# A decoder step on one core: its first modulation in two groups of feature blocks, the second tile ahead of the first keys, and the key work one slot later

## The chip, the cores and the metric

The kernel runs on one core of one Trainium2 chip. The metric is the device time of one execution in microseconds (us). The kernel before takes 1119.65 us, the median of three runs (1116.27 to 1120.73).

The engines are TensorE (PE; its weight loads are listed as PEld), VectorE (DVE), ScalarE (ACT), GpSimd (POOL) and SyncE (SP). Each works through its own queue in order and waits at semaphores for the others. SP, ACT and POOL issue the DMA transfers.

## The reference, cut to what matters

One step of a decoder with one layer, for a prompt (512 tokens) and eight sample sequences of four tokens each. The same weights serve both.

```python
def _modulation(c, w_mod, b_mod):
    m = jax.nn.silu(c) @ w_mod + b_mod            # 9 rows x 1024 @ 1024 x 6144
    return jnp.split(m[:, None, :], 6, axis=-1)

sh1, sc1, g1, sh2, sc2, g2 = _modulation(c, w_mod, b_mod)
h = _rmsnorm(x, norm1_w) * (1 + sc1) + sh1
z = h @ w_in                                      # 1024 x 3584
rq, rk, rv, rg, mq, mk, mv = jnp.split(z, SPLITS, axis=-1)
ret_out, ret_s = _retention_branch(...)
moba_out = _rmsnorm(moba_mix(mq, mk, mv), moba_norm_w)
x = x + g1 * (jnp.concatenate([ret_out, moba_out], axis=-1) @ w_out)
h2 = _rmsnorm(x, norm2_w) * (1 + sc2) + sh2
x = x + g2 * ((jax.nn.silu(h2 @ w_gate) * (h2 @ w_up)) @ w_down)
```

For the sample sequences, `moba_mix` reads a paged cache of 32 pages of 128 keys each: it scores the query against all keys, picks three blocks of 256 keys per query and weighs their values.

The shift `sh1` and the scale `sc1` (the first 2048 of the 6144 columns of `w_mod`) are needed before the first input matmul. The others are needed later.

## The kernel before, in words

Features lie on partitions: the 1024 features are eight blocks ("k") of 128. Weights come in chunks of 256 columns (1 MB). The main line of work is a row of tiles, each 128 output columns for all 512 prompt tokens: 28 tiles of the input projection (`half_tile`, twice per tile), 8 of the output projection, then the FFN. For precision each operand is split into a high and a low part, so a tile is 3 matmuls of 128x512 for each of the eight blocks: high by high and low by high weights (L1016, L1017) and high by low weights (L1018). ACT makes the high part (`split_hi`, `stage_hi`), DVE the low one (`split_in_place`, `act_lo`).

The order is written by hand on each engine, in slots: slot s goes with tile s (0 to 27), then come two slots, 30 to 42 the prompt's retention, 43 to 50 the output projection, 51 to 53 the second norm, from 54 the FFN. Each slot also carries one piece of the sample sequences' key work, on every engine: `slot_head(s)` multiplies key group s (`keys`, L1036; 64 groups, eight to a sequence), whose keys POOL gathers, and which DVE has turned (`turn_keys`, L1638); `slot_rest(s)` does what follows for the last finished sequence by s modulo 8: block sums (0), the choice of blocks (1), maxima (2), exponentials (3, `exps` on ACT), turned probabilities (3 and 4), folding of heads (4), denominators (5). Values of group g are weighed in slot g + `LAG`.

The first 2048 modulation columns are eight chunks of 256, computed one after the other through two buffers `raw[0]`, `raw[1]` (L386: SP loads a chunk once PE is done with the one that lay there). For a chunk PE accumulates block k in row group k % 4 of one bank, so that four partial sums of 32 rows lie below one another; `fold_groups` on DVE (L1549, L1551) adds them up with a copy and three additions. After two chunks `turn_mod` (L978) turns them, and `modulation` (L1562) adds the bias. `gains` (L1566) makes (1 + scale) x norm weight for all eight blocks at once. Only then does ACT stage x: PE turns x, which ACT has scaled by the inverse norm (L552), block by block (L991), and ACT applies gain and shift (L627), then makes the high part (L559); DVE makes the low one (L1594).

The two first sample chunks of the input projection (L961 with `asT`) come between blocks 1 and 2. PE then waits for the constants and starts slot 0 with `keys(0)`, which needs the sample queries out of those chunks (a transpose, `block_diagonal`, L1630) and key group 0; tile 0 comes behind it. The sixteen later modulation chunks go through `rawm` in the slots named in `MOD_AT`, and are turned in those of `TURN_AT`:

```python
MOD_AT = [0, 1] + list(range(2, NT, 2)) + [NT - 1]
TURN_AT = [2] + [MOD_AT[n] + 2 for n in range(3, len(MOD_AT) - 1, 2)] + [NT]
```

In the second norm (slots 51 to 53) DVE forms the reciprocal of the mean squares `rb` (L1958), ACT its square root (L851), and DVE and ACT scale and stage eight blocks in turn (L1950, L855). On ACT `slot(51)` stands ahead of a weight split and `slot(52)` between that and the square root.

## Time and profile before

| | before |
|---|---|
| median of three runs | 1119.65 us |
| the profiled execution | 1118.47 us, its span 1116.6 us |
| PE busy | 979.4 us (88%) |
| DVE busy | 656.7 us (59%) |
| ACT busy | 339.4 us (30%) |
| granted clock of PE, mean | 0.927 |
| moved by DMA | 267.01 MB, mean 239 GB/s |

Busy time is a share of the whole span, so it says little on one stage. The rows below give the stages: start times are in us from the span's start, and "idle before" is how long an engine stood before an instruction, with what released it. A granted clock of 1.00 is 2.4 GHz, 0.50 is 1.2 GHz.

### The profile page before, as it was taken

How to read it: one execution, taken by the hardware profiler on the slowest of the kernel's cores; microseconds unless marked ns; L12 is line 12 of the kernel's file. 1: busy time of each engine (PE TensorE's matmuls, PEld its weight loads, DVE VectorE, ACT ScalarE, POOL GpSimd, SP SyncE). 2: the span in 40 equal slices, each digit the busy share in tenths (PEclk: the TensorE clock that was granted, in tenths of full speed). 3: DMA queues.
4: the chain of work that ended last, by engine and by line, in shares of the span. 5: the costliest groups of instructions: out<-in, count | busy, mean ns of one | idle time of the engine just before them, and what ended most of it. 6: DMA issues, size and time to landing. Idle time of an engine off the chain costs nothing.

```text
span 1116.6 us, 20916 instructions
## 1 busy us (share of the span) xinstructions
PE 979.4 (88%) x7847; PEld 684.4 (61%) x7847; DVE 656.7 (59%) x1152; ACT 339.4 (30%) x678; POOL 91.0 (8%) x90
## 2 busy tenths in 40 slices
PE   3669999999999657467987699999999999999996
PEld 1356766766776334244753476767677777777775
DVE  3555775676676487776656657543266555553344
ACT  4331233324224324224214414333234222221113
POOL 0011110000010021101400123000000000000000
PEclk8679999999999788787988689999999999999998
DMA  9846878877777768576888567977847798887662
GB/s 294 303 150 232 309 252 280 294 263 265 272 261 261 229 229 307 189 257 208 267 300 281 188 212 249 276 226 227 272 123 216 193 233 236 226 242 237 202 227 80
DMA packets 220355, 267.01 MB, mean 239 GB/s; under 512 B 12785, under 2 KB 175929, under 8 KB 212066
## 3 DMA queue, kind: packets, MB, share of 16 engines
q1 hardware_dynamic: 111586, 123.21, 35.1%
q10 hardware_dynamic: 99456, 75.38, 22.0%
q0 software_dynamic: 9216, 67.11, 16.8%
q8 instruction: 62, 1.02, 0.4%
q14 instruction: 35, 0.29, 0.1%
HBM read 260.04 MB, written 5.64 MB: 238 GB/s over the span
## 4 chain that ended last, share of the span: by engine, by line
PE 73%; DVE 13%; DMA 5%; DVEq 3%; ACT 3%; issue 2%; SPq 1%; ACTq 0%
PE banks L1001 13%; PE banks L1002 12%; PE banks L1003 12%; PE banks L961 6%; PE banks L1016 4%; PE banks L1036 4%; PE banks L1091 4%; DVE KT L1638 4%; PE banks L1017 4%; PE banks L1018 4%; DMA raw<-in_w_mod 2%; PE banks L1179 2%; DVEq L1539 2%; DMA raw<-in_w_out 1%; PE banks L1164 1%
## 5 line engine op out<-in xcount | busy, mean ns | idle before, releaser
L1001 PE MATMUL banks<-ahi,whi 128*128 128x512 f32 x416 | 170.9, 411 | 0.0
L571 ACT ACTIVATE whi<-raw 128x1024 fp32r<-128x1024 f32 (+1 forms) x76 | 78.7, 1035 | 301.3 <-PE banks L1003 157.5
L1638 DVE STREAM_TRANSPOSE KT<-K 128x2048 f32<-128x2048 f32 x64 | 147.7, 2308 | 37.0 <-PE banks L1036 29.7
L1002 PE MATMUL banks<-alo,whi 128*128 128x512 f32 x416 | 164.2, 395 | 0.0
L1003 PE MATMUL banks<-ahi,rawlo 128*128 128x512 f32 x416 | 164.0, 394 | 0.0
L1601 DVE TENSOR_TENSOR rawlo<-raw,whi 128x1024 fp32r<-128x1024 f32 (+1 forms) x76 | 91.4, 1203 | 61.9 <-ACT whi L571 59.1
L478 POOL DMA_INDIRECT K<-in_cache_k,kidx x64 | 64.7, 1011 | 581.8 <-DVE KT L1638 538.2
L1001 PEld LDWEIGHTS banks<-ahi,whi 128*128 128x128 f32 x416 | 79.6, 191 | 31.5 <-issue 13.6
L1036 PE MATMUL banks<-KT,qbd 128*32 128x128 f32 x2048 | 75.2, 291 | 25.5 <-DVE KT L1638 24.2
L1016 PE MATMUL banks<-ahi,whi 128*128 128x512 f32 x224 | 93.6, 418 | 1.2 <-DVE rawlo L1608 0.9
L1003 PEld LDWEIGHTS banks<-ahi,rawlo 128*128 128x128 f32 x416 | 79.3, 191 | 17.7
L1002 PEld LDWEIGHTS banks<-alo,whi 128*128 128x128 f32 x416 | 79.9, 192 | 15.1
L1017 PE MATMUL banks<-alo,whi 128*128 128x512 f32 x224 | 88.7, 396 | 0.0
L1018 PE MATMUL banks<-ahi,rawlo 128*128 128x512 f32 x224 | 88.6, 396 | 0.0
L1036 PEld LDWEIGHTS banks<-KT,qbd 128*32 128x32 f32 x2048 | 57.7, 116 | 42.5 <-DVE KT L1638 20.9
L1091 PE MATMUL banks<-V,pT 128*32 128x512 f32 x368 | 54.0, 650 | 3.4 <-issue 2.0
L1016 PEld LDWEIGHTS banks<-ahi,whi 128*128 128x128 f32 x224 | 42.6, 190 | 18.3 <-issue 7.6
L1608 DVE TENSOR_TENSOR rawlo<-raw,whi 128x1024 fp32r<-128x1024 f32 x28 | 34.2, 1223 | 30.4 <-ACT whi L564 14.8
L655 ACT ACTIVATE pm<-banks,st 128x128 f32<-128x128 f32 (+3 forms) x32 | 16.6, 522 | 112.4 <-DVE st L1763 112.4
L1018 PEld LDWEIGHTS banks<-ahi,rawlo 128*128 128x128 f32 x224 | 42.8, 191 | 9.7
L1017 PEld LDWEIGHTS banks<-alo,whi 128*128 128x128 f32 x224 | 42.7, 191 | 7.7
L1551 DVE TENSOR_TENSOR xtmp<-xtmp,banks 32x256 f32<-32x256 f32 x90 | 37.5, 417 | 7.0 <-issue 0.4
(304 smaller groups left out, 1447.6 us busy)
## 6 DMA issues: line engine op xcount, KB each, us to landing
V<-in_cache_v SPq DMA_DIRECT2D x184, 256.0 KB
rawm<-in_w_mod ACTq DMA_DIRECT2D x15, 1024.0 KB
zT<-in_cache_v SPq DMA_DIRECT2D x52, 256.0 KB
raw<-in_w_in ACTq DMA_DIRECT2D x12, 1024.0 KB
raw<-in_w_gate ACTq DMA_DIRECT2D x22, 512.0 KB
raw<-in_w_up ACTq DMA_DIRECT2D x22, 512.0 KB
srw<-in_w_gate SPq DMA_DIRECT2D x22, 512.0 KB, 5.4
srw<-in_w_up SPq DMA_DIRECT2D x22, 512.0 KB, 6.7
```

The costliest lines, as they stand in the source:

```text
L571: act.activation(whi[t % 2][:, 0:kd, :], raw[u][:, 0:kd, t % 2 * P:(t % 2 + 1) * P], ACT.Copy).then_inc(s_hi, 1)
L961: last = pe.matmul(out[32 * g:32 * g + 32, 0:CHUNK], lhs(k), rhs[:, k, :], start=(first and k < 4), stop=(final and k >= kd - 4))
L1001: pe.matmul(out[:, :], whi[t % 2][:, k, :], hi(k), start=(first and n == 0), stop=False)
L1002: pe.matmul(out[:, :], whi[t % 2][:, k, :], lo(k), start=False, stop=False)
L1003: last = pe.matmul(out[:, :], low[:, k, :], hi(k), start=False, stop=(final and n == kd - 1))
L1016: pe.matmul(DB[:, :], whi[m % 2][:, k, :], ahi[:, k, :], start=(k == 0), stop=False)
L1017: pe.matmul(DB[:, :], whi[m % 2][:, k, :], alo[:, k, :], start=False, stop=False)
L1018: last = pe.matmul(DB[:, :], wlow[:, k, :], ahi[:, k, :], start=False, stop=(k == KT - 1))
L1036: last = pe.matmul(LG[32 * gq:32 * gq + 32, (g % 4) * P:(g % 4 + 1) * P], qbd[g // NGRP % 2][:, j, :], KTb[:, :, j, :], start=(jj == 0), s ...
L1091: pe.matmul(VO[32 * pg:32 * pg + 32, :], pT[:, n, 32 * pg:32 * pg + 32], bufs[pg][:, :], start=(n == 0), stop=(n == NGRP - 1)).then_inc(s_ ...
L1601: tt(rawlo[u][:, 0:kd, cols], raw[u][:, 0:kd, cols], whi[t % 2][:, 0:kd, :].bitcast(F32), ALU.subtract).then_inc(s_lo, 1)
L1638: dve.transpose(KTb[:, :, :, :], Kb[g % 2][:, :]).then_inc(s_kt, 1)
```

## The change

1. The first modulation is loaded in eight loads of two blocks k each. Loads 0 to 3 carry all 1024 features' rows for columns 0 to 511 of the shift and 0 to 511 of the scale; loads 4 to 7 those for columns 512 to 1023 of both. PE multiplies each load's two blocks by four groups of 256 columns, each group into its own 32 rows of one bank (bank 0 for the first four loads, bank 1 for the others), so no partial sums are left to fold. One copy and two transposes of 128x128 (`early_modulation`, `turn_early`) follow for each group of loads, and `gains` is called for blocks 0 to 3 and 4 to 7 separately.
2. Six of these loads have a buffer of their own (three new ones behind x, `rawm`, both `raw`) and are issued without a wait; the other two wait for loads 0 and 1 to be used. The sample rows are loaded ahead of x. Of x's four row blocks ACT scales two and DVE two.
3. PE turns x's blocks between the loads. Tile 0 takes high and low activations of each block as soon as it is staged, and the low weights at the end. Two modulation chunks (8 and 9) and tile 1 follow, ahead of `keys(0)`.
4. `KEYS = 1`: all key work comes one slot later on every engine; POOL's other work and the end of the sample sequences (`S_END`) are renumbered to match.
5. A later modulation chunk is kept with one copy of 128 rows; its four partial sums are added by PE as it turns them, through the constant `sum_pv`. `MOD_AT` has slot 0 twice and slot 27 no more.
6. Hidden units of the FFN lie in another order in the same two buffers, with their guards one slot later. Some semaphores of the sample retention are merged.

```diff
-LAG = 12
-MOD_AT = [0, 1] + list(range(2, NT, 2)) + [NT - 1]
+KEYS, LAG = 1, 12
+MOD_AT = [0, 0, 1] + list(range(2, NT - 1, 2))
+TURN_AT = [s + 2 for s in MOD_AT[1::2]]
-S_END = NG + LAG
+S_END = KEYS + NG + LAG
...
+    early = [at(ZT + 8192 + 2048 * i, f"early{i}", [P, 2, DM]) for i in range(3)]
+    mod_buffer = early + [two_k(rawm), two_k(raw[0]), two_k(raw[1])] + early[0:2]
...
+        def early_mod(n):
+            q, i = divmod(n, 4)
+            for a in range(2):
+                cols = slice(a * DM + q * 512, a * DM + q * 512 + 512)
+                sp.dma_start(mod_buffer[n][:, :, a * 512:(a + 1) * 512], w_mod_v[:, 2 * i:2 * i + 2, cols]).then_inc(EARLY[n][0], 16)
...
-        with sp.Fori(1, NMA // 2) as i:
-            for u in range(2):
-                sp.wait_ge(s_md, 2 * i + u - 1)
-                chunk(u, w_mod_v, bass.ds((2 * i + u) * CHUNK, CHUNK))
-        for u in range(2):
-            sp.wait_ge(s_md, NMA - 1 + u)
-            chunk(u, w_in_v, slice(COL_OF[u], COL_OF[u] + CHUNK))
+        for n in range(2, 6):
+            early_mod(n)
+        for n in range(6, NMA):
+            sp.wait_ge(s_md, n - 5)
+            early_mod(n)
+        sp.wait_ge(s_md, 5)
+        chunk(0, w_in_v, slice(COL_OF[0], COL_OF[0] + CHUNK))
+        sp.wait_ge(s_md, 6)
+        chunk(1, w_in_v, slice(COL_OF[1], COL_OF[1] + CHUNK))
...
+        def early_mod(n):
+            pe.wait_ge(*EARLY[n])
+            for kk in range(2):
+                for g in range(4):
+                    last = pe.matmul(bank[n // 4][32 * g:32 * g + 32, 0:CHUNK], cT[:, 2 * (n % 4) + kk, :],
+                                     mod_buffer[n][:, kk, CHUNK * g:CHUNK * (g + 1)],
+                                     start=(n % 4 == 0 and kk == 0), stop=(n % 4 == 3 and kk == 1))
+            last.then_inc(s_md, 1)
...
+        pe.wait_ge(s_hi, 1)
+        for k in range(KT):
+            pe.wait_ge(s_hlo, k + 1)
+            pe.matmul(DB[:, :], whi[0][:, k, :], ahi[:, k, :], start=(k == 0), stop=False)
+            pe.matmul(DB[:, :], whi[0][:, k, :], alo[:, k, :], start=False, stop=False)
+        pe.wait_ge(s_lo, 1)
+        for k in range(KT):
+            last = pe.matmul(DB[:, :], rawlo[0][:, k, 0:P], ahi[:, k, :], start=False, stop=(k == KT - 1))
+        last.then_inc(s_ft, 1)
+        mod_chunk(0)
+        mod_chunk(1)
+        half_tile(1, 0)
+        half_tile(1, 1)
         pe.wait_ge(s_const, 16)
-        for s in range(NT):
+        slot_head(1)
+        mod_chunk(2)
+        slot_rest(1)
+
+        for s in range(2, NT):
...
         def slot_head(s):
+            s -= KEYS
...
         def keep_mod(n, src):
-            dve.wait_ge(s_md, n + 1)
-            fold_groups(mst[0:32, CHUNK * (n % 2):CHUNK * (n % 2 + 1)], src, s_mev)
+            dve.wait_ge(s_md, NMA + n + 1)
+            then(cp(mst[:, CHUNK * (n % 2):CHUNK * (n % 2 + 1)], src[:, 0:CHUNK])).then_inc(s_mev, 1)
```

The first place where rows move is PE's queue between the modulation and tile 0. `raw_81` and `raw_82` are `raw[0]` and `raw[1]`, `cT` holds the turned conditioning vectors, `asT` the sample rows. Before:

```order
L961 MATMUL banks<-raw_82,cT 32x256 x8
L978 MATMUL banks<-ct,mst 128x32 x4
L1140 MATMUL banks<-ct,sq 128x32 x8
L991 MATMUL banks<-ct,xP 128x128 x8
L961 MATMUL banks<-raw_81,asT 32x256 x8
L961 MATMUL banks<-raw_82,asT 32x256 x8
L991 MATMUL banks<-ct,xP 128x128 x24
L1036 MATMUL banks<-KT,qbd_72 32x128 x16
L1016 MATMUL banks<-ahi,whi_85 128x512
```

The same place now, from the end of the first group of loads to tile 0:

```order
L1025 MATMUL banks<-ct,mst 128x128 x2
L1202 MATMUL banks<-ct,sq 128x32 x8
L1030 MATMUL banks<-ct,xP 128x128 x8
L1183 MATMUL banks<-raw_81,cT 32x256 x8
L1183 MATMUL banks<-raw_82,cT 32x256 x8
L1030 MATMUL banks<-ct,xP 128x128 x8
L1183 MATMUL banks<-early_95,cT 32x256 x8
L1030 MATMUL banks<-ct,xP 128x128 x8
L1183 MATMUL banks<-early_96,cT 32x256 x8
L1025 MATMUL banks<-ct,mst 128x128 x2
L1030 MATMUL banks<-ct,xP 128x128 x4
L993 MATMUL banks<-raw_81,asT 32x256 x8
```

The turns of x (L991, now L1030) have moved in among the loads of the second group, and a second pair of transposes (L1025) stands two blocks of x before the first sample chunk.

The second place is PE's queue from the end of tile 0 to tile 2 (`rawm` and `early_97` hold modulation chunks). Before, from tile 0's last matmul to the first of tile 1:

```order
L1018 MATMUL banks<-ahi,rawlo_83 128x512
L961 MATMUL banks<-rawm,cT 32x256 x8
L1036 MATMUL banks<-KT,qbd_72 32x128 x16
L1016 MATMUL banks<-ahi,whi_86 128x512
L1017 MATMUL banks<-alo,whi_86 128x512
```

Now tile 0's end and the beginning of tile 1:

```order
L1260 MATMUL banks<-ahi,rawlo_83 128x512 x8
L993 MATMUL banks<-rawm,cT 32x256 x8
L993 MATMUL banks<-early_97,cT 32x256 x8
L1053 MATMUL banks<-ahi,whi_86 128x512
L1054 MATMUL banks<-alo,whi_86 128x512
```

And tile 1's end and the beginning of tile 2:

```order
L1055 MATMUL banks<-ahi,rawlo_83 128x512
L1073 MATMUL banks<-KT,qbd_72 32x128 x16
L993 MATMUL banks<-rawm,cT 32x256 x8
L1073 MATMUL banks<-KT,qbd_72 32x128 x16
L1053 MATMUL banks<-ahi,whi_85 128x512
```

Key groups 0 and 1, which stood before tiles 0 and 1, stand together before tile 2, with one modulation chunk between them.

The third place is ACT's queue in the second norm, with what each row waits for (`rb` is the root of the mean squares, `pe_x` are the sample exponentials, `whi` a weight chunk's high part). Before:

```order
L846 ACTIVATE stage_55<-x2T 128x512 [waits x2_sums,tile_evicted+2]
L595 ACTIVATE pe_x,sm<-lgs,sm 128x4x32 [waits probs_turned,exp_bias]
L595 ACTIVATE pe_x,sm<-lgs,sm 128x4x32 x7
L599 ACTIVATE sm<-sm 128x32
L588 ACTIVATE lgs<-banks 128x512 [waits exps,logits]
L571 ACTIVATE whi_85<-raw_82 128x1024 [waits tile_done+2,w_loaded1]
L607 ACTIVATE pT<-banks 128x128 [waits page_used,probs_turned]
L607 ACTIVATE pT<-banks 128x128 x3
L851 ACT_TABLE_LOAD
L851 ACTIVATE rb<-rb 128x512 [waits x2_inverse]
```

Now:

```order
L874 ACTIVATE stage_55<-x2T 128x512 [waits x2_sums,tile_evicted+2]
L594 ACTIVATE whi_85<-raw_82 128x1024 [waits tile_done+2,w_loaded1]
L618 ACTIVATE pe_x,sm<-lgs,sm 128x4x32 [waits probs_turned,exp_bias]
L618 ACTIVATE pe_x,sm<-lgs,sm 128x4x32 x7
L622 ACTIVATE sm<-sm 128x32
L611 ACTIVATE lgs<-banks 128x512 [waits exps,logits]
L879 ACT_TABLE_LOAD
L879 ACTIVATE rb<-rb 128x512 [waits x2_inverse]
```

The weight split now comes before the exponentials, and nothing but the copy of the logits is left between them and the square root. The copies of the turned probabilities (L607) have moved behind the third staged block.

## Rows read from the trace of the kernel before

**Rows 1.** The page's slices: 40 equal parts of the span, PE's busy tenths.

```profile
PE   3669999999999657467987699999999999999996
```

**Rows 2.** Short windows: busy us of PE, PEld, DVE, ACT, POOL, clock, DMA share, GB/s.

```profile
6.00:8.00 2.00, 0.00 (x0) 0.00 (x0) 0.00 (x0) 0.00 (x0) 0.00 (x0) 1.00 1.08 354
48.00:50.00 2.00, 2.00 (x25) 0.80 (x17) 1.36 (x3) 0.81 (x2) 0.00 (x0) 0.64 1.05 429
58.00:60.00 2.00, 0.62 (x3) 0.22 (x2) 1.21 (x2) 1.97 (x4) 0.00 (x0) 0.50 0.00 0
```

**Rows 3.** The chain of waits, 0 to 180 us: start, us, what.

```profile
15.39 7.44 DMA raw<-in_w_mod
...
32.60 6.35 DMA raw<-in_w_mod
...
75.53 7.04 DMA rawm<-in_w_mod
```

**Rows 4.** Timeline, 0 to 100 us: start, us, engine, line, operation, count, idle before.

```profile
17.97 1.06 ACT L542 ACTIVATE sq<-xP 128x1024 f32<-128x1024 f32 x1
...
25.50 4.25 ACT L552 ACTIVATE xP<-xP,st 128x1024 f32<-128x1024 f32 x4
...
39.00 1.94 PE L961 MATMUL banks<-raw,cT 128*32 128x256 f32 x16 [0.99 <-DMA raw<-in_w_mod]
...
41.49 1.40 DVE L1551 TENSOR_TENSOR mst<-mst,banks 32x256 f32<-32x256 f32 x3
...
44.02 0.23 DVE L1566 SCALAR_TENSOR_TENSOR gain<-mT,vT 128x72 f32<-128x72 f32 x1 [0.15 <-issue]
...
46.07 0.78 ACT L627 ACTIVATE stage<-banks,mT,gain 128x512 f32<-128x512 f32 x1 [0.69 <-PE banks L991]
...
60.80 0.69 DVE L1594 TENSOR_TENSOR alo<-stage,ahi 128x512 fp32r<-128x512 f32 x1 [0.64 <-ACT ahi L559]
...
63.37 2.31 DVE L1638 STREAM_TRANSPOSE KT<-K 128x2048 f32<-128x2048 f32 x1
...
67.69 0.80 PE L1016 MATMUL banks<-ahi,whi 128*128 128x512 f32 x1
...
74.39 1.07 PE L961 MATMUL banks<-rawm,cT 128*32 128x256 f32 x16
...
76.27 0.50 PE L1016 MATMUL banks<-ahi,whi 128*128 128x512 f32 x1
...
82.08 0.60 ACT L633 ACTIVATE zT<-banks 128x512 f32<-128x512 f32 x1 [4.96 <-PE banks L1018]
...
95.83 0.50 PE L1016 MATMUL banks<-ahi,whi 128*128 128x512 f32 x1
```

**Rows 5.** PE's waits by releaser, 76 to 160 us: total, times, longest.

```profile
PE banks L961 <- DVE mst L1551: 1.9, 1, 1.9
```

**Rows 6.** The same, 300 to 400 us.

```profile
PE banks L978 <- DVE mst L1551: 2.7, 1, 2.7
```

**Rows 7.** The chain of waits, 530 to 700 us.

```profile
553.85 16.70 DMA raw<-in_w_out
...
571.84 3.27 DVEq L1644
```

**Rows 8.** Timeline of ACT and of DVE in the second norm.

```profile
599.55 0.51 ACT L595 ACTIVATE pe_x<-lgs,sm 128x128 f32<-128x128 f32 x1
...
602.63 0.30 ACT L599 ACTIVATE sm<-sm 128x32 f32<-128x32 f32 x1
...
605.35 1.28 ACT L851 ACT_TABLE_LOAD   x1
...
606.64 0.63 ACT L851 ACTIVATE rb<-rb 128x512 f32<-128x512 f32 x1
...
605.40 1.23 DVE L1601 TENSOR_TENSOR rawlo<-raw,whi 128x1024 fp32r<-128x1024 f32 x1
...
608.41 1.29 DVE L1950 TENSOR_TENSOR stage<-x2T,rb 128x512 f32<-128x512 f32 x2
```

More of the change, by code:

```diff
@@ L96, in constants @@
     put("pad0", np.zeros((P, 6)))
+    put("sum_pv", (p % 32)[:, None] == np.arange(32)[None, :])
     put("ones", np.ones((P, P)))
@@ L1134, in slot_rest, with turn_x_early @@
                 fold(b - 1)
-        pe.wait_ge(s_xsn, 1)
-        for k in range(KT):
-            last = pe.transpose(DB[:, k * S:(k + 1) * S], sq[0:S, k * P:(k + 1) * P], ident[0:S, 0:S])
-        last.then_inc(s_xst, 1)
-        pe.wait_ge(s_xn, 1)
-        for k in range(KT):
+        def early_mod(n):
[6 more added lines that the diff above has]
+            last.then_inc(s_md, 1)
+        def turn_x_early(k):
             if k >= 2:
@@ L1588, in _, with early_modulation @@
-        dve.drain()
-        gains(8, V_N1)
+        def early_modulation(group):
+            dve.wait_ge(s_md, 4 * group + 4)
+            then(cp(mst[:, CHUNK * group:CHUNK * (group + 1)], bank[group][:, 0:CHUNK])).then_inc(s_mev, 1)
+            dve.wait_ge(s_mtp, group + 1)
+            for h in range(2):
+                pick = lambda x: x.rearrange("p (a q k h) -> p a q k h", a=2, q=2, k=2)[:, :, group, :, h]
+                dst = mT[:, 0:16, :].rearrange("p (a q k h) s -> p a q k h s", a=2, q=2, k=2)[:, :, group, :, h, :]
+                last = then(tt(dst, SB[:, h * P:(h + 1) * P].rearrange("p (a k r) -> p a k r", a=2, k=2)[:, :, :, 0:NSEQ],
+                               pick(vT[:, 0:16]).unsqueeze(3).broadcast_to((P, 2, 2, NSEQ)), ALU.add))
+            last.then_inc(s_mp, 1)
@@ new lines, in _ @@
+        dve.reciprocal(st2[0:S, 12:13], st2[0:S, 12:13])
+        dve.drain().then_inc(s_rin, 1)
+        dve.wait_ge(s_rst, 1)
+        for i in range(2, TT):
+            last = ts(xP[:, i, :], xP[:, i, :], st2[:, i:i + 1], None, ALU.mult)
+        last.then_inc(s_xn, 1)
+        early_modulation(0)
+        gains(0, 4, 8, V_N1)
+        dve.wait_ge(s_pt, 16)
+        dve.wait_ge(s_ident, 16)
+        for g in range(GRP):
+            q = slice(32 * g, 32 * g + 32)
+            last = ts(kidx[q, :], pt[q, :].rearrange("p (n g) -> p n g", g=GRP)[:, :, g], 32.0, C("row32")[q, :], ALU.mult, ALU.add)
@@ L1591, in act_lo @@
+        last.then_inc(s_idx, 1)
         def act_lo(k, n):
```

302 lines of the change are left out of this document (167 added, 135 removed).

## The prediction

> **What bounds the kernel now.** I read the slices of the span first. TensorE (PE) is at nine tenths or more almost everywhere, except in the first three slices, in a valley in slices 14 to 19 and in slices 22 and 23 [rows 1]. So only work that shortens the time before PE fills up, or those two valleys, can move the end; the change is in the first 100 us.
>
> There the short windows show what is idle. The DMA engines are full while a load is queued (354 GB/s with share 1.08 at 6 to 8 us, 429 at 48 to 50), but stand at share 0.00 at 58 to 60, where PE works 0.62 of 2.00 us at the lower of its two clocks, granted 0.50 [rows 2]. The chain of waits says what that beginning consists of: waits for modulation loads (7.44 and 6.35 us, and 7.04 for a later one), since a buffer is refilled only after PE has used it [rows 3]. Then the timeline shows an almost serial path: last modulation chunk at 39.00, four fold additions, gain at 44.02, staging of feature block 0 at 46.07, block 7's low part at 60.80, the first key transpose at 63.37, tile 0 at 67.69, tile 1 at 76.27, tile 3 at 95.83 [rows 4]. My milestone is the start of tile 3: after it both programs run the same work in nearly the same order.
>
> **The start, step by step.** All from rows, kept apart by engine.
>
> *Loads.* They are the same bytes (eight of 1.05 MB), now six in flight without a wait. Small loads, x and four of them are 6.75 MB: at 354 GB/s from 3 us on that is 3 + 19.1 = 22.1, with half a us to land 22.6. All eight: 10.95 MB, 33.9. Both input chunks, constants, two more modulation chunks and two key gathers: 17.7 MB, 53.0 at 354 and 49.8 if what follows 33.9 runs at 429; I take 51. The Trainium skill (DMA: Bandwidth & Descriptors, "Where 436 GB/s comes from") gives both ends a name: a fabric ceiling of 435 GB/s and a share of about 358 of the HBM for one core. The trace has windows at either number [rows 2]; by the first alone the last of the 17.7 MB would land at 49.5, by the second alone at 52.8; the sum holds neither.
>
> *First group.* x's squares started at 17.97, behind those of the sample rows, which now load first: 0 to 1.8 us sooner, I take 1. The scaling of four row blocks took 4.25; ACT now does two (2.1) and DVE two. That DVE operation is not in the trace; it is bounded by 0 and by the 1.23 of DVE's subtraction of two tiles of that size [rows 8]; I take 1.1 each, hidden beside ACT's two. So x is ready near 25.5 - 1 + 2.1 = 26.6 [rows 4]. Load 3 is used by 22.6 + 1.94 = 24.5; one copy and two transposes (0.4 each) and the additions (0.2 each, with drains) put the first gain near 27. PE then turns the sample rows and block 0, about 1.0 each (gain at 44.02, staging at 46.07): staging starts at 28.3 to 28.9, I take 28.3.
>
> *Second group.* PE's order is now what counts: turns 0 and 1, loads 4 and 5, turns 2 and 3, load 6, turns 4 and 5, load 7. At the low clock the five turns after block 0 and the four loads are 5 x 1.0 + 4 x 1.94 = 12.8 us, and with copy, transposes, additions and gain (2.3) the second gain comes at 43.4; if the clock rises once PE works without gaps, as it has begun to in the window at 48 to 50 (granted 0.64 with PE at 2.00 of 2.00) [rows 2], a load costs 1.07 and a turn half, staging (0.78 + 0.6 a block) becomes the limit in between, and it comes at 37.6. I take 39.0, nearer the high clock. The loads themselves (33.9) are no limit then.
>
> *Tile 0.* Four blocks of staging, 1.35 each (0.78 and some 0.6), and the low part (0.69): last block at 39.0 + 5.4 + 0.7 = 45.1. The two sample chunks lie in between (done 43.4), 16 matmuls of 0.23 (24 of them make tile 1) follow (47.1), and the eight with the low weights, ready at 46.4, end at 49.0. Modulation chunks 8 and 9 (1.07 each): the second waits for its load at 51, done 52.1.
>
> *Tiles 1 and 2.* Tile 1 is 5.6 us (76.27 to its copy at 82.08): 57.7. From 46.4 on DVE has two folds of sample columns (0.5 + 1.40 each), a split (1.23), the block diagonal (61.5 to 63.37) and the first key transpose (2.31), 9.2 us in all, so to 55.6; keys 0 follow tile 1 at once (1.0). Chunk 10's load is asked for at 52 and lands at 57 (5 us, between the 3.0 that 1.05 MB need at 354 GB/s and the 7.04 of such a load [rows 3]); the chunk ends near 59.7. Keys 1 wait for a 2.31 us transpose that can start only after keys 0: 61.9. Tile 2, with a turn in it, 6.0; chunk 11 and keys 2, 2.0: tile 3 starts at 70, against 95.83. Every hand-over between engines costs a little (0.1 to 0.2) and I have left out a dozen: 71.5. The start brings -24.3.
>
> **What the rest adds.**
> - The folding of a modulation chunk becomes one copy: three additions, 1.40 us of DVE, go [rows 4]. Where DVE has slack this is worth nothing. One fold stands in PE's way, a 1.9 us wait [rows 5]: -1.4. The last chunk leaves slot 27, with the 2.7 us that its turning waited [rows 6], and its 1.0 us of PE was already paid at the start: -3.7.
> - Keys one slot later: the last group falls into the FFN, where PE has no idle time: +1.0.
> - The shifted slot also moves a sequence's exponentials (599.55 to 602.9 in one of them: 3.3 us of ACT) [rows 8] from slots 27, 35, 43, 51 to 28, 36, 44, 52. In slot 28 turning the probabilities now waits for half of them: +2.
> - In 51 the last of them began at 602.63, while DVE was still at the reciprocal of x's norms, so they cost nothing. In 52 they stand between the exponent bias, which DVE can give only after its 1.23 us split at 605.40, and the table load (1.28) and square root (0.63), which ran at 605.35 and 606.64 [rows 8]. So: bias at 607.1, exponentials 610.4, a copy of logits (about 0.6) 611.0, load and root 612.9; DVE takes up scaling at 613 instead of 608.41: +4.6. The head fold that filled DVE's time there (between the split's end at 606.6 and 608.41) moves to slot 53, on the path: +1.7; a small reduction leaves: -0.4. Together +5.9.
> - The chain waits from 571.84 on for block sums that stood in DVE's queue behind a split held up by a 16.70 us load, and behind a key transpose (3.27 together) [rows 7]; PE's next tile needs the transpose, not the sums (1.1 each, two of them, and two small operations). They come one slot later, beside a tile: -3. The load's own wait stays.
> - Retention, slots 30 to 42, is bound by DVE: the same operations but one fall in it, at other places. 0, from -5 to +5.
> - Waits on the regrouped semaphores, the permuted hidden units and the constant block change no duration; units are guarded one or two slots after the pages that lay there are used, by the order of the slots: 0, up to +2.
>
> Sum: -24.3 - 1.4 - 3.7 + 1.0 + 2.0 + 5.9 - 3.0 = -23.5. The profiled execution took 1118.47 (span 1116.6), 1.2 below the median 1119.65: 1095.0 profiled, 1096 as median.
>
> **Rivals.**
> 1. *PE's queue is slow at the start.* Everything to the second gain runs at the low clock: 43.4 instead of 39.0, tile 0 pays part of its 24 matmuls at twice 0.23, and the tiles then wait for chunk reloads that collide with key gathers (7.04 us for one in the chain of waits [rows 3]). Tile 3 at 78: gain 18, so 1103. For: the clock granted is 0.64 still at 48 to 50, and 0.50 again at 58 [rows 2]. Against: from 27 us on PE would have hardly a gap.
> 2. *More is gained.* Retention and slot 52 cost nothing, as ACT runs the exponentials before DVE asks: -23.5 - 5.9 - 3 = 1087.
> 3. *It does not do what it says.* If x's normalisation, not the loads, releases the first tile (it ends at 29.75 in the trace), only the fill between 44 and 68 is shortened: tile 3 near 83, with +6 behind it: 1112. Against: x is ready 15 us before it is used now.
> 4. *Slower.* The out-of-phase key work: in retention each slot's transpose (2.31) would fall outside its cover, PE to DVE to PE. It decides from 1.9 us in each of 13 slots; at 2.3 it is +30, at 1125. For: PE is idle half of that time. Against: DVE's sum there is the same, and the semaphores between keys and transpose keep their distance.
>
> **How the numbers follow.** The forecast 0.64 (1090 to 1102), rival 1 0.18, rival 2 0.10, rival 3 0.05, rival 4 0.03. The range for 8 in 10 cuts the outer part of rival 2 and ends above rival 1, whose price has a spread of 5: 1085 to 1108. Within 0.5% (1114 to 1125, about what a measurement of this kernel can tell) lie a bad rival 3 and half of rival 4: 0.04; slower by more 0.02; faster by more 0.94.
>
> **What would show it.** First staging at 28, second gain near 39, DMA share near 1.0 until about 50 with no hole at 22, 30 and 38; tile 0 ending near 49, tile 3 starting near 71; no PE wait on the modulation copy after tile 15; the square root of x's norms after the exponentials, PE's gap there 6 us longer; a smaller gap where the output projection's load is late. I am wrong if tile 3 starts after 80, or if the stretch from there to the end grows by more than 5 us.

## The result, and the profile after

| | before | changed |
|---|---|---|
| median of the comparison | 1118.53 us | 1130.67 us (1127.92 to 1134.33, 4 runs) |
| ratio | 1 | 1.0096, 95% interval 1.0058 to 1.0135 |
| profiled execution, span | 1118.47, 1116.6 us | 1130.31, 1128.5 us |

The change made the kernel about 1% slower; the forecast was 1096, with a chance of 0.02 for slower by more than 0.5%. The slices of the changed kernel's span, with the clock granted to TensorE, answer to [rows 1]:

```profile
PE   3799999989988765767994898999999999999996
...
PEclk8899999989999977678997888999999999999999
```

The weak first slices have shrunk from three to two, but slices of eight tenths stand where the kernel before had nine (the 8s at slices 9, 12, 13 and 25), and the valley is wider. The start itself came out almost as it was worked out. The timeline of the changed kernel, 22 to 74 us, answers to [rows 4] (start, duration, engine, line, operation):

```profile
22.86 1.42 DVE L1678 TENSOR_SCALAR xP<-xP,st 128x1024 f32<-128x1024 f32 x2 [1.13 <-ACTq L573]
...
27.42 0.20 DVE L1666 SCALAR_TENSOR_TENSOR gain<-mT,vT 128x36 f32<-128x36 f32 x1
28.12 0.78 ACT L655 ACTIVATE stage<-banks,mT,gain 128x512 f32<-128x512 f32 x1 [1.98 <-PE banks L1030]
...
36.93 0.20 DVE L1666 SCALAR_TENSOR_TENSOR gain<-mT,vT 128x36 f32<-128x36 f32 x1
...
44.36 0.69 DVE L1692 TENSOR_TENSOR alo<-stage,ahi 128x512 fp32r<-128x512 f32 x1 [1.32 <-ACT ahi L582]
49.54 0.60 ACT L661 ACTIVATE zT<-banks 128x512 f32<-128x512 f32 x1 [4.26 <-PE banks L1260]
...
52.68 1.94 PE L993 MATMUL banks<-early,cT 128*32 128x256 f32 x16 [1.83 <-DMA early<-in_w_mod]
...
61.01 0.60 ACT L661 ACTIVATE zT<-banks 128x512 f32<-128x512 f32 x1 [4.74 <-PE banks L1055]
...
73.98 0.50 PE L1053 MATMUL banks<-ahi,whi 128*128 128x512 f32 x1
```

Tile 3 starts at 73.98, 21.9 us ahead of the kernel before. What follows takes that lead away: from there to the end of the span the kernel before needs 1020.8 us and the changed one 1054.5, which is 33.7 more, where the forecast had 0.8. This table holds four profiled executions at the same places, one of each kernel; the third kernel, introduced below, is the changed one with the work on the keys back in its old slots, and the fourth is the best one found.

| place | before | changed | keys in old slots | best |
|---|---|---|---|---|
| tile 0 copied | 74.50 | 49.54 | 50.50 | 50.00 |
| tile 16 copied | 230.93 | 208.14 | 216.15 | 219.06 |
| tile 26 copied | 346.46 | 337.79 | 331.85 | 335.01 |
| decays of the last retention pair | 486.27 | 485.75 | 471.20 | 469.40 |
| second norm, first scaled block | 608.41 | 605.73 | 586.27 | 584.72 |
| first gate of the FFN | 637.68 | 635.43 | 615.35 | 605.08 |
| first down projection block added | 994.26 | 1004.69 | 971.98 | 963.42 |
| span | 1116.6 | 1128.5 | 1094.0 | 1087.2 |

The lead of the changed kernel is 22.8 us at tile 16, 8.7 at tile 26, 0.5 at the last decays, 2.3 at the first gate; at the down projection it is a lag of 10.4. The kernel with the keys in old slots leads the one before by 14.8 us at tile 16, 14.6 at tile 26 and 15.1 at the last decays, and by 22.1 to 22.3 at the three places behind them.

### The profile page after: what moved, and what is told of

Same layout as the page of the kernel before. It is cut to its first block, busy times and chain, and to the rows that moved or that the text cites. A ratio compares the mean times of both kernels' runs of the same rounds, so it can differ in the third digit from the quotient of the medians.

```text
span 1128.5 us, 20778 instructions
## 1 busy us (share of the span) xinstructions
PE 990.3 (88%) x7867; PEld 695.0 (62%) x7867; DVE 629.2 (56%) x1077; ACT 337.3 (30%) x676; POOL 88.5 (8%) x90
## 4 chain that ended last, share of the span: by engine, by line
PE 69%; DVE 12%; ACT 5%; DMA 4%; DVEq 3%; issue 3%; SPq 1%; ACTq 1%
PE banks L1040 12%; PE banks L1042 11%; PE banks L1041 11%; PE banks L993 5%; PE banks L1053 4%; PE banks L1073 4%; PE banks L1128 4%; PE banks L1054 3%; PE banks L1055 3%; DVE KT L1736 3%; DVEq L1628 2%; DMA early<-in_w_mod 2%; PE banks L1248 1%; ACT pe_x L618 1%; DMA raw<-in_w_up 1%
## 5 line engine op out<-in xcount | busy, mean ns | idle before, releaser
L1699 DVE TENSOR_TENSOR rawlo<-raw,whi 128x1024 fp32r<-128x1024 f32 (+1 forms) x76 | 93.9, 1235 | 68.2 <-ACT whi L594 65.5
L1073 PE MATMUL banks<-KT,qbd 128*32 128x128 f32 x2048 | 76.4, 295 | 28.1 <-DVE KT L1736 25.1
L1040 PEld LDWEIGHTS banks<-ahi,whi 128*128 128x128 f32 x416 | 79.8, 192 | 33.9 <-issue 12.4
L1042 PEld LDWEIGHTS banks<-ahi,rawlo 128*128 128x128 f32 x416 | 79.4, 191 | 17.7
L1073 PEld LDWEIGHTS banks<-KT,qbd 128*32 128x32 f32 x2048 | 58.6, 118 | 46.1 <-issue 23.5
L1706 DVE TENSOR_TENSOR rawlo<-raw,whi 128x1024 fp32r<-128x1024 f32 x28 | 34.3, 1225 | 36.8 <-PE banks L993 23.5
```

The lines of the kernel that those rows point to most:

```text
L1040: pe.matmul(out[:, :], whi[t % 2][:, k, :], hi(k), start=(first and n == 0), stop=False)
L1042: last = pe.matmul(out[:, :], low[:, k, :], hi(k), start=False, stop=(final and n == kd - 1))
L1073: last = pe.matmul(LG[32 * gq:32 * gq + 32, (g % 4) * P:(g % 4 + 1) * P], qbd[g // NGRP % 2][:, j, :], KTb[:, :, j, :], start=(jj == 0), s ...
L1699: tt(rawlo[u][:, 0:kd, cols], raw[u][:, 0:kd, cols], whi[t % 2][:, 0:kd, :].bitcast(F32), ALU.subtract).then_inc(s_lo, 1)
```

## The experiments

**1. Only the keys' slot put back, and only the keys' slot moved.** First the start in groups, with the keys where they were. Besides the constant, keys 2 come behind tile 2's first half, and GpSimd's helpers one gather later. Keys 0 and 1 stay behind tile 1 with a modulation chunk between them, as in the changed kernel; the text on record below says that keys 0 stand ahead of tile 1, which this edit does not do. On TensorE (cut):

```
-KEYS, LAG = 1, 12
+KEYS, LAG = 0, 12
...
+        slot_head(0)
+        mod_chunk(2)
         slot_head(1)
-        mod_chunk(2)
-        slot_rest(1)
```

> The changed kernel, with the work on the keys taken back to the slots that it has before the change (keys 0 ahead of tile 1, keys 1 with tile 1, keys 2 after the first half of tile 2; POOL's helpers too); the start in groups of two k stays. Phase theory (the shift by one slot sets the 8-slot cycle of the keys against the pairs of slots in which weight chunks and hidden units are split, and gives back some 30 us): the start's gain is kept, less 3 to 5 us that tile 1 loses behind keys 0 again; ratio to the kernel before about 0.982 (1098 to 1102 us), and the milestones keep a lead of 18 us or more at tile 16, tile 26 and the first decays. Rival (the loss comes from the early start itself: loads and gathers that run ahead meet other transfers, or a lower granted clock): 1.00 to 1.01, as in the changed kernel, with the lead lost at the same tiles 17 to 26.

Measured: 1095.88 us (1092.65 to 1098.72, 5 runs) against 1120.15, ratio 0.9789 [0.9756, 0.9823]. The time is that of the phase theory, a little better; the lead of 18 us or more at tiles 16 and 26 is not: it is 14.8 and 14.6 (19.6 at the first decays).

The counterpart is the kernel before with the slot moved and its start left alone, with the renumbering of GpSimd's work and the hidden units' order and guards that go with the slot (cut):

```
-LAG = 12
+KEYS, LAG = 1, 12
...
-S_END = NG + LAG
+S_END = KEYS + NG + LAG
```

> The kernel before with the work on the keys one slot later in every slot (and the guards and unit places that go with it), its start otherwise as it was. Phase theory: keys 0 leave the way of tile 0 (a gain of some 5 us), then the shift costs 25 to 32 us: ratio 1.018 to 1.024 (1138 to 1145 us), with the loss at tiles 17 to 26, at the first decays and in the FFN. Rival (early start itself is what costs): 0.995 to 1.003.

Measured: 1154.1 us, ratio 1.03 [1.0266, 1.0334], more than either theory had. So the two halves of the change add up: the start in groups, with the rest of the change but the slot, brings 24 us (1120.15 to 1095.88), and the later keys cost 34, on the old start (1120.15 to 1154.1) and on the new (1095.88 to 1130.67). The second pair has the same order of hidden units on both sides, so the slot costs 34 without any change of that order. The rival, that the early start brings its own loss, falls. On the old start the loss also lies in the same places: in that trace the lag grows by 17.4 us from tile 3 to tile 26, by 12.0 from there to the last decays, and by 12.4 from the first gate to the down projection.

In the kernel with the keys in old slots tile 3 is copied at 86.28, in the changed one at 79.79. I do not take this for a gain of the shift. TensorE waits there for modulation chunk 11, and the lower clock follows; a kernel with the keys late (experiment 4, split ahead) meets the same wait and copies tile 3 at 85.71. The two, in this order:

```profile
76.03 1.94 PE L993 MATMUL banks<-rawm,cT 128*32 128x256 f32 x16 [3.69 <-DMA rawm<-in_w_mod]
...
75.59 1.94 PE L993 MATMUL banks<-rawm,cT 128*32 128x256 f32 x16 [5.15 <-DMA rawm<-in_w_mod]
```

Nor are the 24 us all made at the start. In the profiled executions the lead is 15.4 us when tile 3 is copied and 15.1 at the last decays; 7 more come in the output projection. In the kernel before a load of its weights took 16.70 us there (the chain of waits), and TensorE stood 4.8 us behind it and what follows it. In the kernel with the keys in old slots it took 12.06, with the same sums in VectorE's queue behind it. The load in that kernel, then TensorE's waits from the first to the last block of the projection, before and in that kernel:

```profile
538.24 12.06 DMA raw<-in_w_out
...
PE banks L1055 <- DVEq L1650: 4.8, 1, 4.8
...
PE banks L1092 <- DVEq L1751: 0.2, 1, 0.2
```

Why the load is shorter no run shows.

**2. Where the shift costs.** In the kernel with the keys in old slots one slot P is left without a step of the keys, and all later steps come one slot late (cut, here for 28).

```
+PAUSE = [28]
...
+key_slot = lambda s: -1 if s in PAUSE else s - sum(p < s for p in PAUSE)
...
-            s -= KEYS
+            s = key_slot(s)
```

> The start in groups of two k with the keys in their slots of before up to slot 27; no step of the keys in slot 28, and all their steps one slot late from there to the end. By the two profiles of the kernels that differ in the slot of the keys alone, the late keys lose some 6 us in tiles 17 to 27, 9 in the retention pairs, 6 at the second norm and 13 in the FFN. If the loss belongs to the phase in which each step stands, this kernel is spared the first term only: about 1123 us (1118 to 1128), 1.003 of the kernel before. Rival (the loss is made in the first 28 slots, and the later lags only follow from it): about 1098 to 1104, 0.98 to 0.986.

> As the kernel in which the keys pause in slot 28, but the pause stands in slot 43, the first of the output projection, so that input and retention run with the keys in their slots of before. Phase theory with the retention as a place of loss of its own (9 us): 1118.3 less 4 to 9, 1109 to 1114 us, 0.990 to 0.994 of the kernel before. Rival (the retention costs nothing net, the loss after a pause at 28 is all at the second norm and in the FFN): 1116 to 1120 us, as with the pause at 28.

> As the last, but the keys pause in slot 54, the first of the FFN, so that input, retention, output projection and second norm run with the keys in their slots of before. Phase theory: only the FFN's term is left, 13 us over the kernel without a shift: about 1109 us (1105 to 1113), 0.990 of the kernel before. Rival (FFN loses only because the earlier phases left it late): within 3 us of the kernel without a shift, 1093 to 1099.

| pause in slot | first of | median | ratio to before |
|---|---|---|---|
| none | | 1095.88 | 0.9789 [0.9756, 0.9823] |
| 54 | the FFN | 1098.3 | 0.9811 [0.9761, 0.9862] |
| 43 | the output projection | 1110.53 | 0.9924 [0.9893, 0.9956] |
| 28 | two slots before the retention | 1118.29 | 0.9998 [0.9969, 1.0027] |
| (changed kernel) | the whole program | 1130.67 | 1.0096 [1.0058, 1.0135] |

The loss is spread over all phases: 12.4 us by the slots up to 27, 7.8 by the retention, 14.6 by all that stands from slot 43 on. The rows were measured at different times, when the kernel before took 1118.53 to 1121.09; by the ratios the three parts are 11, 8 and 15. The pauses at 28 and 43 came out as forecast, the one at 54 came out 11 us under its forecast, and the trace says why. From the first scaled block to the first gate this kernel needs 19.3 us (589.15 to 608.49), the one without a pause 29.1 (586.27 to 615.35): one key step less has to pass between the norm and the first FFN tile, where TensorE has nothing else to do (its waits for turned keys in this stretch are one of 7.4 us, and two of 12.2 together in the kernel without a pause). Within the FFN that lead is lost again: 8.0 from the first gate to the down projection (364.6 against 356.6) and 1.8 behind it. So the FFN does have a price for the shift, about 10 here and 12.6 up to the down projection in the changed kernel, and I had overlooked that the empty slot is worth 10 at that place.

**3. The FFN: parity, or the steps of the samples?** Hidden units come in pairs of slots, so I first took it for parity and paused twice (slots 54 and 55).

> The keys pause in slots 54 and 55, so that in the FFN they stand two slots late: the same parity against the pairs of slots of a hidden unit as before the change. Parity theory: the loss of the FFN is gone, 1095 to 1101 us, 0.978 to 0.983 of the kernel before. Rival (each slot of delay costs, by the work that it pushes to the end): at least twice the cost of one slot, 1115 us or more; or, if only the position against the steps of the samples (which do not move with the keys) matters, between the two, 1103 to 1112.

Measured: 1102.04 us, ratio 0.9836 [0.9783, 0.989], between the ranges of the two theories. Two slots are not cheaper than one: from the first gate to the down projection this kernel needs 365.0 us, the one with a single pause 364.6, the one without 356.6. So parity falls as the cause in the FFN. (All keys two slots late would have tested it in every phase, but in that kernel the engines come to wait for one another, one of them for the turned values, so it has no time.) What does not move with the keys are the samples' eight retention steps; they were moved as well, first with the pause at 54, then in the changed kernel:

```
-R_SAMPLE = R_FFN
+R_SAMPLE = R_FFN + 1
```

> As the kernel in which the keys pause in slot 54 (1098.3 us), with the eight retention steps of the samples one slot later too (from slot 55), so that in the FFN keys and samples stand to each other as before the change, and both one slot later against the hidden units. If the FFN's loss (12 us behind a gain of 10 in the pause itself) comes from the position of the keys' steps against the samples': 1086 to 1092 us. Rival (from their position against the hidden units' pairs of slots): no change, 1096 to 1101.

> The changed kernel with the eight retention steps of the samples one slot later (slots 55 to 63). If the FFN's loss comes from the position of the keys against the samples' steps: 8 to 12 us faster than the changed kernel, 1118 to 1122 us. Rival (the hidden units' pairs of slots): no change, 1127 to 1133.

Measured: 1091.14 us (1089.06 to 1093.64), ratio 0.974 [0.9683, 0.9796], the fastest kernel of this study, ahead of the one with the pause alone and of the one with the keys in old slots; and 1121.39, ratio 1.002 [0.9985, 1.0055], 9 us under the changed kernel. The windows from the FFN's beginning to the first down projection block show it in busy time of PE, PEld, DVE, ACT and POOL, granted clock, DMA share and GB/s. First the kernel with the keys in old slots:

```profile
615.00:972.00 357.00, 354.58 (x2462) 257.95 (x2454) 194.58 (x346) 108.64 (x184) 15.97 (x13) 0.99 0.77 223
```

The changed kernel, over the whole stretch and then from the FFN's second gate to its third:

```profile
635.00:1005.00 370.00, 361.55 (x2494) 262.57 (x2487) 198.22 (x350) 108.12 (x183) 16.91 (x14) 0.97 0.76 218
...
653.00:684.00 31.00, 28.37 (x327) 20.38 (x323) 20.74 (x34) 5.27 (x8) 6.61 (x4) 0.78 0.54 167
```

The changed kernel with the samples' steps one slot later, the same two:

```profile
636.00:995.00 359.00, 353.62 (x2477) 257.33 (x2467) 195.41 (x349) 105.82 (x181) 16.90 (x14) 0.99 0.78 225
...
653.00:676.00 23.00, 23.00 (x282) 17.86 (x270) 14.18 (x25) 3.22 (x5) 4.53 (x2) 0.85 0.70 223
```

TensorE idles 8.5 us in the 370, 2.4 in the 357. Its busy time is 7 to 8 us longer than in the other two, for nearly the same matmuls (against the keys in old slots, one key group of about 1 us more). The rest goes with the clock: cut into pieces of 1 us, the changed kernel's FFN stands at 1.2 GHz for 23.9 us, the one with the keys in old slots for 10.2, the one with the samples late for 6.8. A slower matmul counts as busy, and so about half of this loss is in no list of waits.

Not all of it stands behind idle pieces. In the changed kernel the clock is low at 653 to 664, with TensorE listed as busy all the time before and during it; the kernel before and the other two kernels compared here have such a piece near there too, of 6 to 7 us. It is low again at 681 to 690, behind a wait of 2.0 us and through one of 1.4, and at 831 to 834, behind one of 2.8. But behind 2.5 us without work the kernel with the samples late kept 1.00. The changed kernel in the first and third piece, then the other one in and behind its gap:

```profile
657.00:660.00 3.00, 3.00 (x35) 1.64 (x38) 2.16 (x3) 0.00 (x0) 2.15 (x1) 0.50 0.02 5
831.00:834.00 3.00, 3.00 (x8) 2.35 (x8) 2.59 (x7) 0.59 (x1) 0.00 (x0) 0.50 0.72 180
...
819.00:822.00 3.00, 0.53 (x4) 0.40 (x4) 1.52 (x3) 2.49 (x3) 0.00 (x0) 1.00 0.41 119
822.00:825.00 3.00, 3.00 (x14) 2.45 (x14) 2.59 (x7) 0.12 (x1) 0.00 (x0) 1.00 0.90 230
```

**4. The input tiles.** The keys' cycle has eight slots, and the block sums (its first step) fell in even slots before and in odd ones now, where ScalarE splits the next weight chunk behind the attention's probabilities. The timeline of the changed kernel in slot 17:

```profile
213.98 2.31 DVE L1736 STREAM_TRANSPOSE KT<-K 128x2048 f32<-128x2048 f32 x1 [0.16 <-issue]
...
216.21 1.18 DVE L1740 TENSOR_REDUCE sm<-lgs 128x8 f32<-128x1024 f32 x1
...
217.31 1.21 DVE L1741 TENSOR_REDUCE sm<-lgs 128x8 f32<-128x1024 f32 x1
...
220.51 0.17 DVE L1870 TENSOR_SCALAR st<-st 128x2 f32<-128x2 f32 x1
...
220.72 0.37 ACT L683 ACTIVATE pm<-banks,st 128x128 f32<-128x128 f32 x1 [10.11 <-DVE st L1870]
...
222.53 1.06 ACT L587 ACTIVATE whi<-raw 128x1024 fp32r<-128x1024 f32 x1 [0.52 <-ACT stage L672]
...
223.69 1.23 DVE L1706 TENSOR_TENSOR rawlo<-raw,whi 128x1024 fp32r<-128x1024 f32 x1 [3.01 <-ACT whi L587]
...
224.47 0.66 PE L1248 MATMUL banks<-mvtok,pmT 128*128 128x64 f32 x4 [1.13 <-ACT pmT L690]
...
224.97 0.50 PE L1053 MATMUL banks<-ahi,whi 128*128 128x512 f32 x1
```

The next tile's first matmul stands at the end of this chain: two sums of 1.2 us each, row maximum, probabilities (ACT waited 10.11 us), split, low part. Ahead of it in TensorE's queue stands the attention's L1248, and it waits for copies that ACT makes behind the same split. Two edits were made in the changed kernel. In slots 17 and 25 the sums go behind the row maxima, `negmax(n)` (cut):

```
+LATE = (17, 25)
...
-            if 0 <= b < NB_SEQ and t == 0:
+            if 0 <= b < NB_SEQ and t == 0 and s + KEYS not in LATE:
...
                 negmax(n)
+            if s in LATE:
+                block_sums((s - KEYS) // NGRP - 1)
```

> The changed kernel, with VectorE's sums of the key blocks placed behind the row maxima in slots 17 and 25 alone. If it is the block sums ahead of the row maxima that hold ScalarE's probabilities and, behind them, its split of the next weight chunk, the loss at tiles 17 to 26 shrinks by 6 to 13 us: 0.990 to 0.995 of the changed kernel. Rival (the loss there is that of the higher load per slot, whatever the order): within 0.3% of the changed kernel.

Measured: 1126.64 us (10 runs), ratio to before 1.0057 [1.0024, 1.0089]: 4 us less, under the 6 to 13 expected, and the interval overlaps the changed kernel's. In the trace tiles 3 to 26 take 253.3 us, 4.7 less than in the changed kernel. And in every odd slot the split goes ahead of the probabilities (cut):

```
+            if s % 2 and s + 1 < NT:
+                ...
+                split_hi(s + 1)
             if n >= 0:
                 probs(n)
             ...
-            if s % 2 and s + 1 < NT:
-                ...
-                split_hi(s + 1)
```

> The changed kernel, in whose odd input slots ScalarE splits the next weight chunk ahead of the probabilities of the prompt's attention, not behind them. If in slots 17 and 25 the split waits behind probabilities that wait for VectorE's row maxima behind the block sums, the loss at tiles 17 to 26 shrinks by 4 to 9 us: 0.992 to 0.996 of the changed kernel (1121 to 1126 us). Rival (the row maxima and probabilities are the critical ones, and are now held by the split of about 1 us in 14 slots): no gain, or up to 5 us of loss.

Measured: 1123.78 us (12 runs), ratio 1.0024 [0.9994, 1.0054], 7 us less; between the copies of tiles 3 and 26 this kernel takes 248.6 us, the changed one 258.0, the one with the keys in old slots 245.6. So some 9 of the input's 12 us hang on the split behind the probabilities. (The time gained is less than the 9, for this kernel's tile 3 came 5.9 us late, by the wait for chunk 11 shown in experiment 1.) The same edit where the sums stand in even slots:

> The kernel without a shift of the keys (1095.9 us), in whose odd input slots ScalarE splits the next weight chunk ahead of the attention's probabilities. If the split is held only where the block sums stand in an odd slot (as in the changed kernel, where this edit gave 6 us), it brings nothing here: 1092 to 1098 us. Rival (the split is late in every odd slot): 1088 to 1091.

Measured: 1098.28, ratio 0.9796 [0.9753, 0.9839]: nothing, so the order on ScalarE only matters where the sums hold the row maxima. The windows of tiles 15 to 27, of the kernel before, with its sums in even slots:

```profile
217.00:371.00 154.00, 146.73 (x1363) 102.29 (x1361) 107.14 (x204) 52.99 (x152) 11.24 (x12) 0.99 0.79 267
```

and of the changed kernel:

```profile
196.00:359.00 163.00, 151.45 (x1355) 106.68 (x1347) 96.92 (x180) 49.11 (x134) 11.27 (x12) 0.97 0.71 239
```

and of the one with the keys in old slots, which has the changed kernel's operations and the sums in even slots:

```profile
202.00:353.00 151.00, 147.80 (x1365) 104.65 (x1363) 97.73 (x182) 52.37 (x150) 11.27 (x12) 0.99 0.77 259
```

VectorE has the same work in the last two, 97 to 98 us, 10 less than before, since the folds are gone; the changed kernel still takes 9 us more than the one before and 12 more than the one with the keys in old slots. How much an engine has to do is not what holds it, but what stands in front of what.

**5. The retention pairs.** In slot 33, now the first of a pair, VectorE's sums and TensorE's block gates stand ahead of the pair's scores and decays. They were put behind them (cut: first TensorE's two places, then VectorE's; `R_PAIR` is 30):

```
-            if tail and t == 0:
+            if tail and t == 0 and s + KEYS != R_PAIR + 3:
                 block_gates(b)
...
+            if hp == 1:
+                block_gates(3)
...
-            if 0 <= b < NB_SEQ and t == 0:
+            if 0 <= b < NB_SEQ and t == 0 and s + KEYS != R_PAIR + 3:
                 block_sums(b)
...
+            if hp == 1:
+                block_sums(3)
```

> The changed kernel, with the block sums of slot 33 on VectorE behind the decays of the second retention pair, and TensorE's block gates of that slot behind the pair's scores. If it is these sums, now in the first slot of a pair ahead of its scores and decays, that cost the retention, 3 to 6 us of its 9 come back there: the lead at the second decays grows by as much, 0.995 to 0.997 of the changed kernel (1125 to 1128 us). Rival (the loss is spread over all the steps that have moved): less than 2 us at the second decays, same total.

Measured: 1128.62 us (1125.02 to 1133.72), 2 under the changed kernel, which is within the spread of either, and just above the 1125 to 1128 expected. TensorE's waits for these sums and gates in the retention, 380 to 490 us, in the changed kernel:

```profile
PE banks L1100 <- DVE sm L1775: 6.8, 1, 6.8
...
PE banks L1092 <- DVEq L1748: 3.1, 1, 3.1
```

and in this one:

```profile
PE banks L1100 <- DVE sm L1777: 5.4, 1, 5.4
PE banks L1092 <- DVEq L1750: 4.6, 1, 4.6
```

The second pair's decays come 5.2 us sooner against its own first decays, as expected; in the next pair 3.4 of them are lost, where the gates' wait has grown to 4.6 us in its new place; at the last pair's decays the kernel is 4.3 ahead, and 3.6 at the first scaled block of the norm. So these sums are one of the causes in the trace, though the medians do not resolve it, and the wait is passed on in part. The rest of the 8 us of the retention is located and not traced.

**6. The second norm.** Two kernels differ in one step of the keys alone, which takes the last set of exponentials with it: the best kernel with its pause in 52 has that step in slot 51, with its pause in 51 in slot 52.

> As the best kernel so far (pause in slot 54, steps of the samples one slot later, 1091.1 us), but with the pause in slot 52: the exponentials of the keys stay in slot 51, ahead of the second norm's root, and the two norm slots hold one step of the keys, not two. The key step that VectorE does between the norm and the first FFN tile comes back, its cost (some 3 to 5 us by the wait for KT there) less the one saved in slot 52: 1089 to 1096 us.

> As the last, but with the pause in slot 51, so that the same exponentials stand in slot 52, as in the changed kernel, between the norm's root and its scaled tiles. By the norm step of the forecast (5.9 us) this is 5 to 7 us slower than with the pause in 52. Rival (TensorE's work on the keys covers them): within 2 us of it.

Measured: 1096.6 us, ratio 0.9808 [0.9751, 0.9864], and 1103.35, ratio 0.9876 [0.9816, 0.9937]: 6.8 us, in the 5 to 7 expected; the first of the two came out just above its 1089 to 1096. ScalarE's timeline in the first, last exponential, table and root:

```profile
580.61 0.30 ACT L624 ACTIVATE sm<-sm 128x32 f32<-128x32 f32 x1
...
582.65 1.28 ACT L881 ACT_TABLE_LOAD   x1
583.95 0.63 ACT L881 ACTIVATE rb<-rb 128x512 f32<-128x512 f32 x1
```

and in the second:

```profile
583.53 0.52 ACT L620 ACTIVATE pe_x<-lgs,sm 128x128 f32<-128x128 f32 x1 [7.21 <-DVE sm L1788]
...
586.62 0.31 ACT L624 ACTIVATE sm<-sm 128x32 f32<-128x32 f32 x1
...
587.73 1.28 ACT L881 ACT_TABLE_LOAD   x1
589.02 0.63 ACT L881 ACTIVATE rb<-rb 128x512 f32<-128x512 f32 x1
```

The exponentials waited 7.21 us for their bias, which VectorE gave at 583.26, right behind its split of 1.23 us, and the root came 5.1 us later (6.6 against the start of VectorE's reciprocal). From the first scaled block to the first gate the kernel with the pause in 52 needs 28.1 us, the best one, with the pause in 54, 20.4: the empty slot in front of the FFN once more.

## Why the prediction was wrong, point by point

- *The start: right, in sum and in most of its parts.* First staging 28.12 (forecast 28.3), second gain 36.93 (39.0, in 37.6 to 43.4), last low part 45.05 (45.1), tile 0 copied 49.54 (49.0), tile 1 copied 61.01 (57.7), tile 3 from 73.98 (71.5). VectorE's scaling of a row block took 0.75 (two in 1.42), not 1.1. Tile 1 is late because modulation chunk 9 started at 52.68, and its matmuls and the tile's first ones ran at the lower clock (0.50 at 54 to 56). The chunk ended at 54.6, not 52.1, and that is the 2.5 us by which tile 3 is late. Rivals 1 and 3 are out: tile 3 starts at 73.98, not at 78 or 83, and the lead there is 21.9 of the 24.3 forecast. That the whole kernel without the shift is 24.3 us faster is luck as a check of this term: its lead is 15.4 at tile 3, and the output projection adds 7.
- *The load of 17.7 MB* was taken at 51, between 49.8 and 53.0; the DMA share was 0.97 at 49 to 50 us, 0.28 and 0.11 in the next two, and the wait ended at 52.68. By the two rates that the Trainium skill names (DMA: Bandwidth & Descriptors, "Where 436 GB/s comes from"), applied to what follows 33.9, the estimate is 49.5 or 52.8; the trace lies by the second, but its last 2 us are a tail in which most DMA engines stand idle, not a rate, and the window of 429 GB/s [rows 2] says that the second is no ceiling here.
- *Second norm: right.* +5.9 forecast, 5.1 at the root and 6.8 at the end by experiment 6; +5.2 between the kernels before and changed, from the last output block to the first gate.
- *The output projection: its sign right, its mechanism not shown.* The forecast had -3, by block sums that move away from behind the late load, and "The load's own wait stays". From the first to the last block the changed kernel gained 5.5 on the one before, and its chain of waits holds neither the sums nor the load. But the kernel with the keys in old slots, whose sums stand where they stood, gained 6.5 in the same place. So the load's wait did not stay, and the gain does not need the moved sums; the shift on the old start gained 4.7 with a load of 14.73 us, so moving them may be enough too.
- *Behind tile 3: where the forecast failed.* It took the milestone at tile 3 because "after it both programs run the same work in nearly the same order", and gave all that follows +0.8 (-23.5 less -24.3). It measured +33.7, and the experiments put 34 on the later keys. The steps that failed are the next three, in the order of time.
- *Input tiles: the step that failed first.* The sum had -1.4, -3.7 and +2 here. The folds' waits did go (TensorE has none for the modulation copy left), but no term stood for the sums' move from even slots to odd ones. Between tiles 3 and 26 the late keys cost 12 us, 9 of which hang on the split behind the probabilities that wait for the sums. I had read the key steps of slots 27 and later for what moved, and none in the tiles before.
- *"Retention ... 0, from -5 to +5": failed.* The reason given, the same operations at other places, is what does not hold. From the last input tile to the last decays the changed kernel lost 11.3 us to the one before; the experiments give 7.8. One cause is shown in a trace (experiment 5), the rest stays open.
- *"Keys one slot later: +1.0" in the FFN: failed.* It counted TensorE's work of one group, 1.0 us, and not that the keys' steps now meet other steps of the samples: 12.7 us lost between the first gate and the down projection, of which 10 come back in the trace, and 9 in the median, when the samples move too (experiment 3).
- *Rival 4* is nearest: out-of-phase key work, with the end 1125. Its mechanism was too narrow. It saw the transpose leave its cover in 13 slots of the retention; what happened is that steps once in eight slots (sums, exponentials) came ahead of work on the path, shown in the input tiles and the second norm and for a part of the retention, that in the FFN the keys' steps met the samples', and that TensorE ran longer at its lower clock (23.9 us of the FFN against 10.2). With a chance of 0.03 it was valued by its one place, not by the number of places where the same question stood.

In sum, against the kernel before, in the profiled executions: 22.8 us ahead at tile 16, then 14.1 lost to tile 26, 3.1 gained in the last tile, 11.3 lost to the last decays, 2.2 gained by the second norm's first scaled block (7.0 to the output projection's end, less 4.8 at the norm), 0.4 lost to the first gate, 12.7 in the FFN and 1.5 behind it: 11.9 behind in the span.

## What to carry to other kernels

- A periodic side job that is woven into a main loop has a phase. Moving it by one slot moves every one of its steps against every periodic step of the main loop (weight chunks every two slots, retention pairs every three, sample steps at fixed places), so a shift of one slot is priced step by step in each phase of the program, never as one more slot of work.
- When a change has a part that is meant to pay and a part that only makes room for it, time them apart: here the first was worth 24 us and the second cost 34, and leaving the second out gave a kernel 2% faster than before. Then look in the trace where each is made: 7 of the 24 came in the output projection, far behind the start that was to bring them.
- Where an engine waits for a side job just ahead of a main phase, an empty slot there can pay more than its lateness costs (10 us at the first FFN tile). It paid only when the samples' steps, which had been aligned with the side job, moved with it: 1098.3 without, 1091.14 with them, against 1095.88 with no pause.

## What the runs showed that I had not expected

- A gap can come with about as much time again at the lower clock. Over the FFN the changed kernel idles 6.0 us more than the one with the keys in old slots and is busy 7.0 more (361.55 against 354.58), with 23.9 against 10.2 us at the lower clock. Yet the clock also fell where no idle time stands before it, and stayed up behind one gap of 2.5 us, so these traces give no rule for when it falls.
- VectorE multiplied a 128 x 1024 tile by a column of scalars in 0.75 us, where its subtraction of two tiles of that size took 1.23. I had taken 1.1, near the second. The Trainium skill (VectorE: DVE Perf Modes, "Mode 2×_2P — use both read ports for one tensor") has a rule for it: with one tensor operand, in SBUF, fp32 too goes at twice the pace, which a subtraction of two tensors cannot; the trace agrees in direction, 0.75 against 1.23, a factor of 1.6.
- The wait for the 17.7 MB ended some 2 us after the DMA engines had gone mostly idle: share 0.28 and 0.11 from 50 to 52 us, and the wait until 52.68. The estimate by rate has no such term; why the last piece is late, no run shows.
- Executions of one kernel scatter by more than several of the effects above: the kernel before took 1113.38 to 1128.4 us in 15 of them, and the changed one with the samples late 1117.75 to 1130.92 in 12. What hangs on 2 to 4 us of a median is weak; the places in the traces carry it.
